# Two float32 transformer blocks on one core: where the projection steps and the reciprocal turns stand inside the attention loops

## The chip, the cores and the metric

The kernel runs on one core of a Trainium2 chip. It is one launch that computes four layers. The metric is the device time of that launch in microseconds (us). The core's engines work side by side and meet only at semaphores: TensorE (PE in the rows, its weight loads PEld), VectorE (DVE), ScalarE (ACT), GpSimd (POOL), and SyncE (SP), which only issues DMAs here.

## The reference

One sequence of 512 tokens of width 1024 passes two blocks of two layers each. Only the attention with 64-wide heads matters here:

```python
# even layer of block 1                      odd layer of block 1: dilated windows, then MLA
qa, ka, va, qd, kd, vd = split_cols(h @ w_in, EVEN_IN_SPLIT)
o_a = moba_attention(heads(qa, 8, 64), heads(ka, 8, 64), heads(va, 8, 64), rel_table[:, :8])
o_b = diff_attention(qd, kd, vd, lam, subln_g, lam_init, ...)   # p[0] - lam * p[1], then rmsnorm of the heads' output
# both layers of block 2
yc = neighbourhood_attention(qc, kc, vc, rpb[l])
gates = jax.nn.sigmoid(gl + b_gate[l]); merged = sum(gates * (ys @ w_branch))
```

In each of them 512 queries meet up to 512 keys, a bias is added, a softmax is taken, and its output is divided by the row sums (`den`). All is float32. A product with a weight is made of three matmuls, of high and low parts: `hh·wh + hl·wh + hh·wl`.

## The kernel before

Every engine's program is written out by hand, and each engine runs its own in the order written. A wait stops everything that stands behind it on that engine.

There are five passes through the function `attention`: moba, diff, dil, and na once in each of two rounds of a loop. A pass has four groups (g = 0 to 3) of two heads and four query tiles, so 32 units. PE, ACT and DVE each count slots t = 0, 1, 2, ... One unit goes through the slots like this:

- PE, even t: `score(t)` and `score(t+1)`, rows `S<-k_sb,q_sb` or `S<-kr_sb,qr_sb`. DVE: bias and row minimum (`biased<-S,...`, L1375). ACT: `soften`, the exponential (`probs<-biased,stats`, L1074), which also waits for PE's transpose of unit t-2.
- PE: transpose of unit t-2 (`T<-ident,probs`, L598). ACT: `copy_turned` of the same unit (`probsT<-T`, L1080), after its `soften(t)`.
- PE, odd units together: the product with V (`O<-probsT,V`, L699; in diff `O<-V,probsT`, L604, each unit for itself).

Between these PE makes the projections for the next group. A **part** is one k step of three matmuls with 512 columns (L470 to L472); eight parts make the queries of the next group in the PSUM bank `PA`, eight more its keys in the bank `PB`. `FILL` says how many parts go into each slot of a group, `last_plan` how many parts of the phase behind (the diff queries and keys, the out projection, the merge gates and the first branch product) go into the slots from 24 on. DVE takes the queries out of PA in the third slot (`take_q`, L1472) and the keys out of PB in the sixth slot (`take_k`, L1477) of the group; `score` of the next group waits for both. When the last part of queries or keys is done, POOL splits the next weights into the free buffer (L450, then L452).

The row sums are inverted token by token, but are wanted along the columns. So at slot `Y_TURN[g]` PE runs `den_turn`: eight pairs of small matmuls (L714) put the reciprocals of group g into a bank, ACT copies the bank one slot later (L1125, "the copy of the reciprocals", `den_copied`), behind its `soften` and `copy_turned` of that slot, DVE multiplies (L1425), ACT and DVE split the result (L1129, L1429). In diff, `y_turn` at the same place transposes the normed output (L724) after DVE's `y_norm` (L1456) in slot 8g + 13.

```python
                for t in range(end + 1):
                    if t < 32 and t % 2 == 0:
                        score(t); score(t + 1)
                    if t in turns:
                        (y_turn if kind == "diff" else den_turn)(b, turns.index(t))
                    for part in parts[sum(slots[:t]):sum(slots[:t + 1])]:
                        part()
```

Of the kernel before, what the change touches and what calls it, by code (L numbers as in the profile page):

```python
# [9 lines left out]
ACT = mybir.ActivationFunctionType  # L10

S = 512
P = 128
DT = 8
# [99 lines left out]

FILL = [3, 3, 2, 2, 3, 3, 0, 0]
Q_AT, K_AT = 3, 6
Y_TURN = {"moba": (15, 23, 27, 35), "diff": (15, 23, 30, 38)}
Y_TURN["dil"] = Y_TURN["na"] = Y_TURN["moba"]

# [70 lines left out]
def build(nc, x_in, weights, consts, cols_in, lam_in, rel_in, rpb_in, strips_rel, strips_na, out):  # L190
    with ExitStack() as ctx:
# [130 lines left out]

        NTABLE, NFIRST = 8, 5

        def flat_y(g):
# [137 lines left out]
        def _(pe):  # L463
# [157 lines left out]

            def qk_parts(b, *bank_free):

                def part(j):
                    if j == DT:
                        pe.wait_ge(*bank_free)
                    qk_part(b, j, j + 1)

                return [lambda j=j: part(j) for j in range(2 * DT)]

            def attention(b, b0, kind, last_parts=(), last_plan=()):
# [5 lines left out]
                parts = sum((qk_parts({**b, **{n: b[n] + m * g for n, m in (("e", 2), ("a", 1), ("b", 1))}},  # L637
                                      *((y_split, 2 * (b["g"] + max(g - 1, 0)) + 1) if kind == "diff" else
                                        (den_copied, b["dc"] + max(g - 1, 0))))
                             for g in range(3)), []) + list(last_parts)  # L640
                slots = FILL * 3 + list(last_plan)
                slots += [0] * (end + 1 - len(slots))
# [61 lines left out]
            def den_turn(b, g):  # L704

                pe.wait_ge(den_ready, b["dr"] + 4 * g + 4)
                if g < 3:
                    pe.wait_ge(pb_taken, b["b"] + min(g + 2, 3) + 1)
                else:
                    pe.wait_ge(o_taken, b["u"] + 24 + 2)  # L710
                for qt in range(QT):
                    for head in range(2):
                        r = rden_of[g % 2][:, 2 * qt + head:2 * qt + head + 1].to_broadcast([P, 64])
                        last = mm((PB if g < 3 else O0)[64 * head:64 * head + 64, qt * P:qt * P + P], r, ident[:, :],  # L714
                                  start=True, stop=True)
                last.then_inc(yt_ready, 2)
# [150 lines left out]
            def gate_part(b, k):  # L867

                if k == 0:
                    pe.wait_ge(pa_taken, b["a"] + 1)  # L870
                    pe.wait_ge(w_split, b["e"] + 3)
                last = three(PA[:, :], wsl(0, k), hs(k), k == 0, k == DT - 1)
                if k == DT - 1:
                    last.then_inc(gate_ready, 1)
# [96 lines left out]
            def moba_stat():  # L971
                pe.wait_ge(table_in, 16 * NTABLE)
                stat(H("moba_v"), False)

            v_projection(H("moba_v"), between=(None, moba_stat, lambda: spread(H("moba_v"))))
            attention(H("moba"), H("moba_q0"), "moba", qk_parts(H("diff_q0"), den_copied, 3),
                      [2, 2, 2, 1, 1, 0, 0, 2, 2, 2, 2])
            v_projection(H("diff_v"))
            o = H("out0")
            first_out = [lambda s=s, k=k: out_part(o, s, k) for s in range(2) for k in range(6)]  # L980
            first_out += [lambda s=s: out_part(o, s, 6) for s in range(2)]
            attention(H("diff"), H("diff_q0"), "diff", first_out, [1, 1, 1, 1, 1, 1, 0, 0, 0, 2, 2, 1, 1, 1, 1])
            out_part(o, 0, 7); out_part(o, 1, 7)
# [10 lines left out]
            qk_part(H("dil_q0"), DT, 2 * DT)  # L994
            attention(H("dil"), H("dil_q0"), "dil")
            pe.wait_ge(kr_done, 1)
# [5 lines left out]
            with pe.Fori(0, LAYERS2) as l:  # L1002
                axial_kv(H("axial_kv", l)); pool_tiles(H("pool", l), H("axial_kv", l), H("axial", l)); axial(H("axial", l))
                qk_part(H("na_q0", l), 0, 2 * DT)
                v_projection(H("na_v", l), True)
                m = H("merge", l)
                first_gate = [lambda k=k: gate_part(m, k) for k in range(DT)] + [lambda k=k: branch_part(m, k) for k in range(4)]
                attention(H("na", l), H("na_q0", l), "na", first_gate, [1] * 12)
                merge(m)
                out_tiles(H("out2", l), lambda k: (mh[:, k, :], ml[:, k, :]), m_split, H("out2", l)["m"], 1)  # L1010
                stat(H("norm_mp", l))
                up(H("up2", l), True); down(H("down2", l))
                stat(H("norm_fp", l))
# [3 lines left out]
        def _(act):  # L1017
# [84 lines left out]
            def attention(b, kind, ytile, early=None):  # L1102
# [3 lines left out]
                for t in range(turns[3] + (2 if kind == "diff" else 4)):  # L1106
# [11 lines left out]
                    if t - 1 in turns:  # L1118
                        g = turns.index(t - 1)
                        act.wait_ge(yt_ready, 2 * (b["g"] + g) + 3)  # L1120
                        if kind == "diff":
                            A(tile(yh, ytile + g), (PB if g < 3 else O0)[:, :], ACT.Copy, scale=scale).then_inc(y_hi, 2)
                        else:
                            act.wait_ge(y_split, 2 * (b["g"] + max(g - 1, 0)) + 1)
                            A(flat_y(g), (PB if g < 3 else O0)[:, :], ACT.Copy).then_inc(den_copied, 1)  # L1125
                    if kind != "diff" and t - 3 in turns:
# [132 lines left out]
        def _(dve):  # L1259
# [219 lines left out]
            def attention(b, kind, ytile, after=None):  # L1479
# [10 lines left out]
                for t in range(turns[3] + (3 if kind == "diff" else 5)):  # L1490
# [20 lines left out]
                    if after is not None and t == 29:  # L1511
                        take_q(after, 0)
                    if after is not None and t == 36:
                        take_k(after, 0)
# [479 lines left out]
```

## Time and profile before

| | |
|---|---|
| median of 3 runs | 3264.05 us (3263.01 to 3266.23) |
| profiled execution: its time | 3260.93 us |
| its span, first to last instruction | 3259.1 us |
| PE busy | 3105.8 us, 95% |
| DVE / ACT / POOL busy | 1481.7 / 788.6 / 1660.0 us |
| mean granted TensorE clock | 0.969 of full speed |
| moba, diff, dil, na, na in the span | from 52, 162, 731, 1547 and 2512 us, 83 to 108 us each |

Times of rows are us from the span's start. An idle time in brackets at a row's end, with a releaser, is how long the engine stood still ahead of it, and what ended that. PE's spans overlap its next instruction's, so a distance is best read from start to start.

### The profile page before, as it was taken

The numbers are of one execution on the slowest core, as the hardware profiler recorded it, in microseconds if no ns is written. First come the engines' busy times: TensorE is split into PE (matmuls) and PEld (weight loads), VectorE is DVE, ScalarE is ACT, GpSimd is POOL, SyncE is SP. The second block draws the span as 40 slices with busy tenths as digits, with TensorE's granted clock in tenths as the row PEclk, the third lists the DMA queues.
The fourth block names the chain that finished last, engine by engine and source line by source line (L and its number), as shares of the span: only waits on it lengthen the run. The fifth ranks groups of instructions, "written<-read, shape, count | busy, mean of one in ns | idle before, by whom it ended". The sixth has DMA issues, their size and how long they took to land.

```text
span 3259.1 us, 44842 instructions
## 1 busy us (share of the span) xinstructions
PE 3105.8 (95%) x14594; PEld 2441.7 (75%) x14594; DVE 1481.7 (45%) x2555; ACT 788.6 (24%) x1425; POOL 1660.0 (51%) x1254
## 2 busy tenths in 40 slices
PE   8998999999899999899999989998899999989997
PEld 6776888876678887667678868887667678868885
DVE  3246444332454433633533476631633433576622
ACT  2343221014322211243421122210142511122201
POOL 4324666662166666312346646665313256646674
PEclk9999999999999999889999989999889999999998
DMA  6251223321022233102312222232102322212232
GB/s 159 78 161 65 94 95 105 105 91 59 26 90 97 97 109 104 36 23 57 93 68 97 87 66 97 96 114 85 40 33 62 75 78 97 90 65 97 97 113 74
DMA packets 99595, 274.79 MB, mean 84 GB/s; under 512 B 38126, under 2 KB 38894, under 8 KB 99490
## 3 DMA queue, kind: packets, MB, share of 16 engines
q1 hardware_dynamic: 97328, 269.07, 25.8%
q10 hardware_dynamic: 2162, 4.36, 0.7%
q8 instruction: 61, 1.00, 0.1%
q14 instruction: 44, 0.36, 0.0%
HBM read 269.66 MB, written 11.54 MB: 86 GB/s over the span
## 4 chain that ended last, share of the span: by engine, by line
PE 71%; DVE 4%; issue 2%; ACT 1%; DVEq 0%; ACTq 0%
PE PA L470 11%; PE PA L471 10%; PE PA L472 10%; PE PB L470 8%; PE PB L472 8%; PE PB L471 8%; PE T L598 2%; PE O L604 2%; PE S L567 2%; PE O L699 1%; PE S L660 1%; PE O L502 1%; DVE hl L1298 1%; DVE tmps L1336 0%; PE PB L759 0%
## 5 line engine op out<-in xcount | busy, mean ns | idle before, releaser
L452 POOL TENSOR_TENSOR wl<-raw,wh 128x1024 fp32r<-128x1024 f32 (+2 forms) x416 | 1126.6, 2708 | 33.4
L449 POOL TENSOR_TENSOR zero<-zero 128x1 f32<-128x1 f32 x416 | 82.7, 199 | 1530.7 <-PE PA L472 799.0
L470 PE MATMUL PA<-hh,wh 128*128 128x512 f32 x1392 | 566.2, 407 | 30.4 <-DVE hl L1298 11.4
L471 PE MATMUL PA<-hl,wh 128*128 128x512 f32 x1392 | 550.1, 395 | 0.0
L472 PE MATMUL PA<-hh,wl 128*128 128x512 f32 x1392 | 549.6, 395 | 0.0
L450 POOL CAST wh<-raw 128x1024 fp32r<-128x1024 f32 (+2 forms) x416 | 476.8, 1146 | 0.0
L470 PEld LDWEIGHTS PA<-hh,wh 128*128 128x128 f32 x1392 | 265.7, 191 | 139.8 <-issue 65.8
L470 PE MATMUL PB<-hh,wh 128*128 128x512 f32 x896 | 358.5, 400 | 0.0
L472 PE MATMUL PB<-hh,wl 128*128 128x512 f32 x896 | 350.4, 391 | 0.0
L471 PE MATMUL PB<-hl,wh 128*128 128x512 f32 x896 | 350.2, 391 | 0.0
L472 PEld LDWEIGHTS PA<-hh,wl 128*128 128x128 f32 x1392 | 266.3, 191 | 57.6
L471 PEld LDWEIGHTS PA<-hl,wh 128*128 128x128 f32 x1392 | 266.4, 191 | 54.0 <-issue 2.2
L1074 ACT ACTIVATE probs<-biased,stats 128x512 f32<-128x512 f32 (+2 forms) x240 | 155.2, 647 | 408.6 <-PE T L598 226.3
L1631 DVE SCALAR_TENSOR_TENSOR tmps<-S,cols,tmps 128x511 f32<-128x511 f32 (+1 forms) x264 | 197.9, 750 | 39.6 <-DVE tmps L1631 19.8
L470 PEld LDWEIGHTS PB<-hh,wh 128*128 128x128 f32 x896 | 169.1, 189 | 47.5 <-issue 14.4
L472 PEld LDWEIGHTS PB<-hh,wl 128*128 128x128 f32 x896 | 168.7, 188 | 36.0
L471 PEld LDWEIGHTS PB<-hl,wh 128*128 128x128 f32 x896 | 169.1, 189 | 33.7 <-issue 1.2
L598 PEld LDWEIGHTS T<-ident,probs 128*128 128x128 f32 x792 | 98.8, 148 | 72.5 <-issue 37.3
L1170 ACT ACTIVATE T<-tmps 128x512 f32<-128x512 f32 x88 | 53.0, 602 | 391.7 <-DVE tmps L1631 391.7
L1298 DVE SCALAR_TENSOR_TENSOR hl<-x,cols,hh 128x512 fp32r<-128x512 f32 (+1 forms) x80 | 129.3, 1622 | 39.0 <-ACT hh L1040 38.8
L470 PE MATMUL PA<-acth,wh 128*128 128x512 f32 x352 | 137.4, 390 | 0.0
L598 PE MATMUL T<-ident,probs 128*128 128x128 f32 x792 | 136.3, 288 | 0.8 <-ACT probsT L1080 0.8
(285 smaller groups left out, 4928.0 us busy)
## 6 DMA issues: line engine op xcount, KB each, us to landing
raw<-in_w_up SPq DMA_DIRECT2D x176, 512.0 KB, 3.4
raw<-in_w_down SPq DMA_DIRECT2D x64, 768.0 KB, 4.2
raw<-in_w_merge SPq DMA_DIRECT2D x48, 768.0 KB, 4.2
raw<-in_w_out SPq DMA_DIRECT2D x32, 512.0 KB, 3.4
strips_na<-in_rpb SPq DMA_DIRECT2D x1, 7620.0 KB, 32.0
raw<-in_w_pool SPq DMA_DIRECT2D x12, 512.0 KB, 3.4
raw<-in_w_na_qk SPq DMA_DIRECT2D x12, 512.0 KB, 3.5
raw<-in_w_na_v SPq DMA_DIRECT2D x8, 512.0 KB, 3.5
```

Of the source, the lines that this page charges most:

```text
L449: nc.gpsimd.tensor_tensor(zero[:, :], zero[:, :], zero[:, :], ALU.add)
L450: nc.gpsimd.tensor_copy(wh[s][:, 0:width], raw[s][:, 0:width]).then_inc(w_head, 1)
L452: nc.gpsimd.tensor_tensor(wl[s][:, 0:width], raw[s][:, 0:width], wh[s][:, 0:width].bitcast(F), ALU.subtract).then_inc(w_split, 1)
L470: mm(dst, h_, rh, start=first, stop=False)
L471: mm(dst, h_, rl, start=False, stop=False)
L472: return mm(dst, l_, rh, start=False, stop=last)
L567: mm(SB[t % 2][:, 0:L], q_sb[r, qt * P:qt * P + P], k_sb[r, 0:L], start=True, stop=True).then_inc(s_ready, 1)
L598: last = nc.tensor.transpose(TB[t % 2][:, k * P:k * P + P], probs[t % 2][:, k * P:k * P + P], ident[:, :])
L604: last = mm(OB[t % 2][:, 0:dv], probsT[t % 2][:, k * P:k * P + P], values(k), start=(k == 0), stop=(k == L // P - 1))
L1074: A(probs[t % 2][:, 0:L], biased[t % 2][:, 0:L], ACT.Exp, scale=-1.0, bias=mn[:, t % 8:t % 8 + 1], accum_out=den[:, t % 8:t % 8 + 1]).then ...
L1298: STT(out=tile(hl, j), in0=tile(x, j), scalar=cols[:, bass.ds(gain_at + j, 1)], in1=tile(hh, j).bitcast(F), op0=ALU.mult, op1=ALU.subtract ...
L1631: ins = STT(out=dst[:, lo:hi], in0=src[:, lo - d:hi - d], scalar=w(k), in1=dst[:, lo:hi], op0=ALU.mult, op1=ALU.add)
```

## The change

Three tables of numbers and the semaphores that go with them. In groups 1 and 2 the parts stand two to a slot and begin in slots 6 and 7 of the group before, which had none (diff keeps one empty slot); `last_plan` begins at slot 22 instead of 24. The reciprocals of groups 0 and 1 are turned in slots 12 and 20 instead of 15 and 23, through PA (the queries' bank) instead of PB, and so the parts that write PA next (queries of group 3 in slot 14, the first part of the phase behind in slot 22) wait for ACT's copy of them. In diff `y_turn` moves from slots 15 and 23 to 16 and 24. DVE's take of the next phase's keys in moba moves from slot 36 to 34.

```diff
-FILL = [3, 3, 2, 2, 3, 3, 0, 0]
+FILL = {"moba": ([3, 3, 3, 3, 2, 2], [2, 2, 2, 2, 2, 2, 2, 2]), "diff": ([3, 3, 3, 3, 2, 2], [2, 2, 2, 2, 0, 3, 3, 2])}
+FILL["dil"] = FILL["na"] = FILL["moba"]
-Y_TURN = {"moba": (15, 23, 27, 35), "diff": (15, 23, 30, 38)}
+Y_TURN = {"moba": (12, 20, 27, 35), "diff": (16, 24, 30, 38)}
...
+        def den_bank(g):
+            return (PA, PA, PB, O0)[g]
...
-            def qk_parts(b, *bank_free):
+            def qk_parts(b, q_free=None, k_free=None):
                 def part(j):
-                    if j == DT:
-                        pe.wait_ge(*bank_free)
+                    if j == 0 and q_free is not None:
+                        pe.wait_ge(*q_free)
+                    if j == DT and k_free is not None:
+                        pe.wait_ge(*k_free)
...
-                                      *((y_split, 2 * (b["g"] + max(g - 1, 0)) + 1) if kind == "diff" else
-                                        (den_copied, b["dc"] + max(g - 1, 0))))
+                                      None if kind == "diff" or g < 2 else (den_copied, b["dc"] + g - 1),
+                                      (y_split, 2 * (b["g"] + g - 1) + 1) if kind == "diff" and g else None)
                              for g in range(3)), []) + list(last_parts)
-                slots = FILL * 3 + list(last_plan)
+                slots = FILL[kind][0] + FILL[kind][1] * 2 + list(last_plan)
...
-                if g < 3:
-                    pe.wait_ge(pb_taken, b["b"] + min(g + 2, 3) + 1)
+                if g < 2:
+                    pe.wait_ge(pa_taken, b["a"] + g + 2 + 1)
+                elif g == 2:
+                    pe.wait_ge(pb_taken, b["b"] + 3 + 1)
...
@@ gate_part (first part of the merge)
                     pe.wait_ge(w_split, b["e"] + 3)
+                    pe.wait_ge(den_copied, b["dc"] - 2)
...
-            attention(H("moba"), H("moba_q0"), "moba", qk_parts(H("diff_q0"), den_copied, 3),
-                      [2, 2, 2, 1, 1, 0, 0, 2, 2, 2, 2])
+            attention(H("moba"), H("moba_q0"), "moba", qk_parts(H("diff_q0"), (den_copied, 2), (den_copied, 3)),
+                      [2, 2, 1, 1, 1, 1, 0, 2, 2, 2, 2])
...
-            attention(H("diff"), H("diff_q0"), "diff", first_out, [1, 1, 1, 1, 1, 1, 0, 0, 0, 2, 2, 1, 1, 1, 1])
+            attention(H("diff"), H("diff_q0"), "diff", first_out, [1, 1, 1, 1, 0, 1, 0, 1, 0, 0, 0, 2, 2, 1, 1, 1, 1])
...
-            attention(H("dil"), H("dil_q0"), "dil")
+            attention(H("dil"), H("dil_q0"), "dil", (), [0, 0])
...
-                attention(H("na", l), H("na_q0", l), "na", first_gate, [1] * 12)
+                attention(H("na", l), H("na_q0", l), "na", first_gate, [2, 2, 1, 1, 1, 1, 0, 1, 1, 1, 1])
...
-                    if after is not None and t == 36:
+                    if after is not None and t == 34:
                         take_k(after, 0)
```

How PE's order changes at three places, row by row of the program (in brackets the semaphores that a row waits for; `S` are the scores, `T` the transposes of the exponentials, `O` the products with V). First, in moba, PE before, from the scores of slot 14 to the first part of slot 16:

```order
L660 MATMUL S<-kr_sb,qr_sb 128x512 [waits s_taken] x2
L598 MATMUL T<-ident,probs 128x128 [waits pt_copied,p_ready]
L598 MATMUL T<-ident,probs 128x128 x2
L699 MATMUL O<-probsT,V 64x128 [waits pt_copied]
L699 MATMUL O<-probsT,V 64x128 x3
L714 MATMUL PB<-ident,stats 64x128 [waits pb_taken,den_ready]
L714 MATMUL PB<-ident,stats 64x128 x7
L598 MATMUL T<-ident,probs 128x128 [waits pt_copied,p_ready]
L598 MATMUL T<-ident,probs 128x128 x2
L660 MATMUL S<-k_sb,q_sb 128x128 [waits s_taken,pb_taken,pa_taken]
L660 MATMUL S<-k_sb,q_sb 128x128 [waits s_taken]
L470 MATMUL PA<-hh,wh 128x512 [waits w_split,pa_taken]
```

and PE of the change in moba, from the last part of slot 13 to the two parts of slot 14:

```order
L474 MATMUL PB<-hh,wh 128x512
L475 MATMUL PB<-hl,wh 128x512
L476 MATMUL PB<-hh,wl 128x512
L602 MATMUL T<-ident,probs 128x128 [waits pt_copied,p_ready]
L602 MATMUL T<-ident,probs 128x128
L666 MATMUL S<-kr_sb,qr_sb 128x512 [waits s_taken] x2
L474 MATMUL PA<-hh,wh 128x512 [waits w_split,pa_taken,den_copied]
L475 MATMUL PA<-hl,wh 128x512
L476 MATMUL PA<-hh,wl 128x512
L474 MATMUL PA<-hh,wh 128x512
L475 MATMUL PA<-hl,wh 128x512
L476 MATMUL PA<-hh,wl 128x512
```

The turn of the reciprocals is gone from slot 15 (it stands in slot 12 now), and slot 14, which had no part, has two, the first of which waits for `den_copied`.

Second, in diff, PE before, slots 14 and 15 up to the first score of slot 16:

```order
L660 MATMUL S<-kr_sb,qr_sb 128x512 [waits s_taken] x2
L598 MATMUL T<-ident,probs 128x128 [waits pt_copied,p_ready]
L598 MATMUL T<-ident,probs 128x128 x2
L604 MATMUL O<-V,probsT 128x128 [waits o_taken,pt_copied]
L604 MATMUL O<-V,probsT 128x128
L724 MATMUL PB<-ident,y_tok 128x128 [waits pb_taken,y_normed]
L724 MATMUL PB<-ident,y_tok 128x128 x3
L598 MATMUL T<-ident,probs 128x128 [waits pt_copied,p_ready]
L598 MATMUL T<-ident,probs 128x128 x2
L604 MATMUL O<-V,probsT 128x128 [waits o_taken,pt_copied]
L604 MATMUL O<-V,probsT 128x128 x2
L660 MATMUL S<-k_sb,q_sb 128x128 [waits s_taken,pb_taken,pa_taken]
```

and of the change, slot 14 and the first rows of slot 15:

```order
L666 MATMUL S<-kr_sb,qr_sb 128x512 [waits s_taken] x2
L474 MATMUL PA<-hh,wh 128x512 [waits w_split,pa_taken]
L475 MATMUL PA<-hl,wh 128x512
L476 MATMUL PA<-hh,wl 128x512
L474 MATMUL PA<-hh,wh 128x512
L475 MATMUL PA<-hl,wh 128x512
L476 MATMUL PA<-hh,wl 128x512
L602 MATMUL T<-ident,probs 128x128 [waits pt_copied,p_ready]
L602 MATMUL T<-ident,probs 128x128 x2
L608 MATMUL O<-V,probsT 128x128 [waits o_taken,pt_copied]
L608 MATMUL O<-V,probsT 128x128
L474 MATMUL PA<-hh,wh 128x512
```

Behind the scores of slot 14 now come two parts of the queries, in slot 15 two more, and they wait for nothing that DVE does in slots 13 to 15; the turn (`PB<-ident,y_tok`) stands behind the scores of slot 16.

Third, in na, PE before at the end of the pass: the transpose of unit 31 (slot 33), a part and the products of units 30 and 31 (slot 34), the last turn and the last part (slot 35):

```order
L598 MATMUL T<-ident,probs 128x128 [waits pt_copied,p_ready]
L598 MATMUL T<-ident,probs 128x128 x3
L470 MATMUL PB<-yh,wh 128x512
L471 MATMUL PB<-yl,wh 128x512
L472 MATMUL PB<-yh,wl 128x512
L699 MATMUL O<-probsT,V 64x128 [waits pt_copied]
L699 MATMUL O<-probsT,V 64x128 x7
L714 MATMUL O<-ident,stats 64x128 [waits o_taken,den_ready]
L714 MATMUL O<-ident,stats 64x128 x7
L470 MATMUL PB<-yh,wh 128x512
L471 MATMUL PB<-yl,wh 128x512
L472 MATMUL PB<-yh,wl 128x512
```

and of the change, from the transpose of unit 30 (slot 32) on:

```order
L602 MATMUL T<-ident,probs 128x128 [waits pt_copied,p_ready]
L602 MATMUL T<-ident,probs 128x128 x3
L705 MATMUL O<-probsT,V 64x128 [waits pt_copied]
L705 MATMUL O<-probsT,V 64x128 x7
L680 REGISTER_ALU
L602 MATMUL T<-ident,probs 128x128 [waits pt_copied,p_ready]
L602 MATMUL T<-ident,probs 128x128 x3
L705 MATMUL O<-probsT,V 64x128 [waits pt_copied]
L705 MATMUL O<-probsT,V 64x128 x7
L723 MATMUL O<-ident,stats 64x128 [waits o_taken,den_ready]
L723 MATMUL O<-ident,stats 64x128 x7
L899 REGISTER_ALU
```

No part is left between the products of units 28 and 29 and the end; the part that stood behind the last turn stands ahead of it now.

## Rows read from the trace of the kernel before

**Rows 1.** The page's head: each engine's busy time, share of the span and instructions.

```profile
PE 3105.8 (95%) x14594; PEld 2441.7 (75%) x14594; DVE 1481.7 (45%) x2555; ACT 788.6 (24%) x1425; POOL 1660.0 (51%) x1254
```

**Rows 2.** Timeline of moba, slots 13 to 15: start, us, engine, line, operation [idle before].

```profile
88.92 0.36 ACT L1080 ACTIVATE probsT<-T 128x256 f32<-128x256 f32 x1
...
89.20 0.55 PE L598 MATMUL T<-ident,probs 128*128 128x128 f32 x3
...
90.75 1.09 PE L714 MATMUL PB<-ident,stats 128*64 128x128 f32 x16 [0.42 <-DVE k_sb L1477]
```

**Rows 3.** Timeline of diff, slots 13 to 16, the turn of slot 23, and slot 29.

```profile
199.33 1.13 PE L660 MATMUL S<-kr_sb,qr_sb 64*128 64x512 f32 x4
...
199.35 3.78 DVE L1456 TENSOR_SCALAR y_tok<-y_tok,stats 128x128 f32<-128x128 f32 x4
...
200.06 2.35 POOL L452 TENSOR_TENSOR wl<-raw,wh 128x1024 fp32r<-128x1024 f32 x1
...
204.51 0.47 ACT L1080 ACTIVATE probsT<-T 128x384 f32<-128x384 f32 x1
...
204.96 1.05 PE L724 MATMUL PB<-ident,y_tok 128*128 128x128 f32 x4 [2.80 <-DVE k_sb L1477]
...
208.54 0.50 PE L470 MATMUL PA<-hh,wh 128*128 128x512 f32 x1
...
232.19 0.97 PE L724 MATMUL PB<-ident,y_tok 128*128 128x128 f32 x4 [2.78 <-DVE kr_sb L1477]
...
248.27 1.25 DVE L1456 TENSOR_SCALAR y_tok<-y_tok,stats 128x128 f32<-128x128 f32 x4
```

**Rows 4.** Stretches behind diff's first turn and na's gap: busy us by engine, PE's granted clock, DMA.

```profile
205.00:208.40 3.40, 3.40 (x17) 3.14 (x17) 1.02 (x5) 1.19 (x3) 0.00 (x0) 0.50 0.39 99
...
2614.80:2621.70 6.90, 6.14 (x15) 4.81 (x16) 1.32 (x3) 2.00 (x2) 3.34 (x1) 0.51 0.33 103
```

**Rows 5.** Timeline of the second na, slots 28 to 35 and the merge's first matmul.

```profile
2599.01 0.50 PE L470 MATMUL PA<-hh,wh 128*128 128x512 f32 x1
...
2599.67 0.59 ACT L1125 ACTIVATE y_tok<-PB 128x512 f32<-128x512 f32 x1
...
2599.81 0.60 PE L598 MATMUL T<-ident,probs 128*128 128x128 f32 x4
...
2606.61 1.09 PE L699 MATMUL O<-probsT,V 128*64 128x128 f32 x16 [0.32 <-ACT probsT L1080]
...
2607.79 0.60 ACT L1080 ACTIVATE probsT<-T 128x512 f32<-128x512 f32 x1 [1.24 <-PE O L699]
...
2609.73 1.09 PE L699 MATMUL O<-probsT,V 128*64 128x128 f32 x16
...
2610.66 1.04 PE L714 MATMUL O<-ident,stats 128*64 128x128 f32 x16
...
2615.56 0.79 PE L470 MATMUL PA<-hh,wh 128*128 128x512 f32 x1 [2.95 <-DVE tmps L1670]
```

**Rows 6.** Timeline of moba, slots 28 and 29, and the two parts of slot 33.

```profile
127.14 0.44 PE L598 MATMUL T<-ident,probs 128*128 128x128 f32 x2
...
127.82 0.59 ACT L1125 ACTIVATE y_tok<-PB 128x512 f32<-128x512 f32 x1
...
134.46 0.50 PE L470 MATMUL PB<-hh,wh 128*128 128x512 f32 x1
...
135.96 0.60 PE L598 MATMUL T<-ident,probs 128*128 128x128 f32 x4
```

**Rows 7.** Timeline of the second na, slots 13 and 14.

```profile
2555.97 0.72 ACT L1074 ACTIVATE probs<-biased,stats 128x512 f32<-128x512 f32 x1 [2.12 <-PE T L598]
...
2556.69 0.57 ACT L1080 ACTIVATE probsT<-T 128x512 f32<-128x512 f32 x1
...
2556.86 0.66 PE L598 MATMUL T<-ident,probs 128*128 128x128 f32 x4
```

**Rows 8.** Timeline of dil, slot 24.

```profile
800.57 1.09 PE L699 MATMUL O<-probsT,V 128*64 128x128 f32 x16 [0.61 <-ACT probsT L1080]
```

More of the change, by code:

```diff
@@ L706, in den_turn @@
                 pe.wait_ge(den_ready, b["dr"] + 4 * g + 4)
-                if g < 3:
-                    pe.wait_ge(pb_taken, b["b"] + min(g + 2, 3) + 1)
+                if g < 2:
+                    pe.wait_ge(pa_taken, b["a"] + g + 2 + 1)
+                elif g == 2:
+                    pe.wait_ge(pb_taken, b["b"] + 3 + 1)
                 else:
                     pe.wait_ge(o_taken, b["u"] + 24 + 2)
+                bank = den_bank(g)
                 for qt in range(QT):
@@ L713, in den_turn @@
                         r = rden_of[g % 2][:, 2 * qt + head:2 * qt + head + 1].to_broadcast([P, 64])
-                        last = mm((PB if g < 3 else O0)[64 * head:64 * head + 64, qt * P:qt * P + P], r, ident[:, :],
-                                  start=True, stop=True)
+                        last = mm(bank[64 * head:64 * head + 64, qt * P:qt * P + P], r, ident[:, :], start=True, stop=True)
                 last.then_inc(yt_ready, 2)
@@ L1124, in attention @@
                             act.wait_ge(y_split, 2 * (b["g"] + max(g - 1, 0)) + 1)
-                            A(flat_y(g), (PB if g < 3 else O0)[:, :], ACT.Copy).then_inc(den_copied, 1)
+                            A(flat_y(g), den_bank(g)[:, :], ACT.Copy).then_inc(den_copied, 1)
                     if kind != "diff" and t - 3 in turns:
```

## Prediction

> **What bounds the kernel now.** I read the page's head first: PE is busy 95% of the span, DVE 45%, ACT 24%, POOL 51% [rows 1]. So only PE's idle time can be won, and every new wait of PE is lost. The timelines of the passes say where the idle time stands and what ends it.
>
> In moba PE stops 0.42 us ahead of the turn in slot 15, for DVE's take of the keys out of PB [rows 2], and as long ahead of slot 23's; dil has the same two. Na has none. In diff the stop in the same places is 2.80 and 2.78 us. The reason stands in two rows there: DVE's `y_norm`, four instructions that take 1.25 us in slot 29, takes 3.78 us in slot 13, while POOL's split of weights (released by the last key part of slot 13) runs from 200.06 to 202.41 [rows 3]. From 205.0 to 208.4 PE is then granted 0.50 of its clock, the 1.2 GHz level [rows 4], and for as long behind the second stop.
>
> The end of na is bound otherwise. PE's last turn starts at 2610.66, ACT and DVE then finish the output, and the merge's second gate projection waits 2.95 us for DVE and starts at 2615.56 [rows 5]. What counts there is when the last turn starts: 4.90 us later the merge goes on. The part behind the turn is free.
>
> **The change part by part**, as the difference of PE's time. A part alone in its slot costs 0.80 us (2599.01 to 2599.81) [rows 5], two cost 1.50 us (134.46 to 135.96) [rows 6]. So a further part costs 0.70 us, and a block of parts has 0.10 us of its own; since PE changes from scores or products to transposes without a block too, I take 0.06 us for a block more. For the waits ACT's order decides: in the slot behind a turn it does `soften`, which waits for PE's transpose in that slot, then `copy_turned`, then the copy of the reciprocals.
>
> *Slot 14 (turn in 12), a new wait for that copy.* In na `copy_turned` of slot 13 ends at 2556.69 + 0.57 = 2557.26 [rows 7]; the copy of a bank takes 0.59 us [rows 5] and ends at 2557.85. PE comes to the place of the part at 2556.86 [rows 7]. Wait: 1.0 us. In moba, with shorter rows: 88.92 + 0.36 + 0.59 = 89.87 against 89.20 [rows 2], 0.67 us; dil the same.
>
> *Slot 22 (turn in 20)*: the same pattern, 1.0 us in na, 0.67 us in moba, nothing in dil, which has no part there.
>
> *Slot 29 (turn in 27, as before)*: PB is written here now instead of in slots 31 (moba) and 32 (na). Moba: the copy ends at 127.82 + 0.59 = 128.41, some 0.1 us on PE sees it, and PE was there at 127.14 [rows 6]: 1.37 us. Na: 2599.67 + 0.59 + 0.1 = 2600.36 against 2599.01 [rows 5]: 1.35 us.
>
> *The end of moba and na, without parts behind slot 32.* The products of units 28 and 29 end at 2606.61 + 1.09 = 2607.70; two copies of 0.60 us must follow before those of 30 and 31 can start, near 2609.0, and PE has one transpose of 0.60 us to do. Idle: 0.7 to 0.9 us, 0.8 taken. Two parts cover it now, and the products start at 2609.73 [rows 5].
>
> *The part behind na's last turn* goes ahead of it: 0.68 us on the path, where it was free.
>
> *Removed*: 0.84 us of stops ahead of the turns in moba and in dil [rows 2], 0.32 us in na (at 2606.61) [rows 5].
>
> *Dil's end* has no parts, and PE waits there for ACT. With the turn of slot 23 gone ahead, the copy of the reciprocals (0.59 us) leaves ACT's slot 24, where PE stood 0.61 us [rows 8]. I take 0.5 us of gain, with bounds of 0 and 1.2 us (both of that copy's and its split's ACT time).
>
> *Diff.* The parts of slots 14 and 15 have another bank and other weights than the stopped turn, so they run while DVE stands. `y_norm` will still meet POOL, since the last key part stays in slot 13; it begins later than now (its ACT work follows a transpose with one part more ahead of it), so it ends some 0.5 us later. From 199.33 [rows 3] I count: scores 1.06, two parts 1.50, transpose and product 1.1, two parts 1.50, transpose 0.5; then the product of unit 12 needs ACT's copy, now done at 204.51 + 0.47 = 204.98, then at 205.5; product, scores and turn bring PE to 207.6. Now the same, without the four parts, is done at 208.54 [rows 3]. Gain: 0.9 + 3.0 = 3.9 us, the slow clock's 1.7 us among it. In slots 22 and 23 only two parts stand in the way, PE waits about 1.9 us for the product of unit 20, and the same count gives 2.4 us. Against that, the key parts of slot 19 wait for DVE's read of the turned output, which is one slot nearer (0.5 us, an estimate by the lengths above; bounds 0 and 1), and 0.1 us of blocks. Diff: 5.7 us won.
>
> Here a rule of the Trainium skill bears. The trace shows `y_norm` stretched to 1 us behind the end of POOL's L452 at 202.41 [rows 3]. "SBUF — State Buffer", section "Who interferes with whom", says that a `tensor_scalar` in a two-port mode and a GpSimd instruction take a shared port pair as an exclusive lock, and the later one blocks for the whole of the other. By that rule the stall stays, and only its cover changes; the trace agrees.
>
> **The sum.** Blocks of parts: moba 27 to 32, dil 18 to 22, na 29 to 32 ahead of the last turn.
> Moba: 2 × 0.67 + 1.37 + 0.8 + 0.3 − 0.84 = +3.0 us.
> Dil: 0.67 + 0.24 − 0.84 − 0.5 = −0.4 us.
> Na: 1.0 + 1.0 + 1.35 + 0.8 + 0.68 + 0.18 − 0.32 = +4.7 us, twice +9.4 us.
> Diff: −5.7 us.
> Together +6.3 us. The profiled execution took 3260.93 us, 1.8 us more than its span, and would take 3267. The median of before is 3264.05, 3.1 us above it; added to that, the sum gives 3270. I say 3269.5, since each wait was counted in full.
>
> All else keeps its cover: the splits of weights that the parts of slots 6 and 14 need are released in slots 2 and 9, and a split takes under 4 us of POOL where four slots take ten; DMAs move with them; DVE and ACT are less than half busy, and while PE waits they catch up.
>
> **Rivals.**
> *The new waits are hidden* (not slower). If ACT were ahead of PE in slots 13, 21 and 28, the waits for `den_copied` would fall out: 3 × 0.67 + 1.37 + 2 × (2.0 + 1.35) = 10.1 us less, so 3264 − 4 = 3260. For it: ACT stands idle 2.12 us ahead of `soften` [rows 7]. Against it: that idle time is a wait for PE's own transpose, and the copy stands behind it in order. It decides from the point where PE has 2 us of work between that transpose and the part; it has the scores, 1.06 us.
> *The clock falls behind the new gaps* (slower still). In diff it fell during gaps of 2.8 us, and once in the 2.95 us gap ahead of the merge, for 6.9 us [rows 4, 5]; the first na kept it. Without the part behind the last turn both gaps are 3.9 us. A fall costs half its time: 1.7 us in diff, 3.4 us in na; one more in na and one in diff that stays make 3270 + 5 = 3275. The Trainium skill, "TensorE: Matmul & The Clock Gate", section "HAM oscillation", says likewise that idle gaps bring the lower level and half the time spent in it is lost; by its rule the first na too would lose its 3.4 us. The trace agrees in three gaps, not in the fourth.
> *Diff gains nothing*: if the parts of slots 14 and 15 waited for weights, or the later turn held DVE back as much as it is relieved, −5.7 becomes 0 and the time 3275. Against it: the weights' split has five slots.
>
> **How the numbers follow.** My forecast (waits as counted, diff covered) 0.5, between 3265 and 3273 by the bounds of dil's end, of slot 19 and of the passes' ends. Waits hidden, wholly or in good part: 0.25, 3257 to 3264. Clock falls: 0.15. Diff gains nothing: 0.1. The range that leaves out 2 in 10 is 3259 to 3276. A measurement of this kernel tells 0.2% (6.5 us) from no change. Slower by more is nearly half of the forecast's share and most of the two slower rivals': 0.42. Faster by more needs the hidden waits and more from diff: 0.15. Within: 0.43.
>
> **What would show it.** Right: rows of PE that write PA in slots 14 and 22 and PB in slot 29 with idle time ahead, ended by ACT's copy, 0.7 to 1.4 us each; no 2.8 us stop in diff and full clock at its first turn; na's last turn some 4.7 us later after the pass's first score; a gap near 3.9 us ahead of the merge. Wrong: those rows without idle time; a turn in slot 12 that waits for the take of the queries; passes of moba and na that end sooner than before.

## The result, and the profile after

The changed kernel takes 3269.86 us (median of 22 runs, 3264.14 to 3274.83); the kernel before took 3265.10 us beside it (22 runs, 3263.01 to 3269.27). The ratio is 1.0014, with a 95% interval of 1.0008 to 1.0021: 4.8 us slower, inside the 0.2% that I called no change. Forecast were 3269.5 us, in a range of 3259 to 3276.

The page's head, as in [rows 1]. PE's busy share has not moved:

```profile
span 3268.5 us, 44834 instructions
PE 3109.4 (95%) x14594; PEld 2443.0 (75%) x14594; DVE 1474.3 (45%) x2555; ACT 788.9 (24%) x1425; POOL 1658.0 (51%) x1254
```

The lines behind the diff stand 4 to 9 numbers further down now: L470 is L474, L699 L705, L714 L723, L724 L732, L1125 L1134, L1375 L1384, L1456 L1465, L1670 L1679.

*Moba.* Timeline, slots 14, 29 and the last products (start, us, engine, line, operation, [idle before and what ended it]). The places are those of [rows 2] and [rows 6]:

```profile
89.63 0.59 ACT L1134 ACTIVATE y_tok<-PA 128x512 f32<-128x512 f32 x1
90.27 0.50 PE L474 MATMUL PA<-hh,wh 128*128 128x512 f32 x1 [0.56 <-ACT y_tok L1134]
...
127.89 0.59 ACT L1134 ACTIVATE y_tok<-PB 128x512 f32<-128x512 f32 x1
128.52 0.50 PE L474 MATMUL PB<-hh,wh 128*128 128x512 f32 x1 [1.41 <-ACT y_tok L1134]
...
139.78 1.09 PE L705 MATMUL O<-probsT,V 128*64 128x128 f32 x16 [0.69 <-ACT probsT L1089]
```

The 0.42 us stop ahead of the turn is gone. In its place the first part behind the turn waits until ACT has copied the reciprocals out of the same bank, in slots 14 and 22 (0.56 us each) and 29. Slot 29 is the dearest, since the copy starts only at 127.89 and PE has stood there since 127.11.

*Second na.* Timeline of the same places, as in [rows 7] and [rows 5]; the last row is the merge's second gate projection:

```profile
2565.89 0.49 PE L474 MATMUL PA<-hh,wh 128*128 128x512 f32 x1 [0.95 <-ACT y_tok L1134]
...
2611.77 0.50 PE L474 MATMUL PB<-yh,wh 128*128 128x512 f32 x1 [1.23 <-ACT y_tok L1134]
...
2619.37 1.09 PE L705 MATMUL O<-probsT,V 128*64 128x128 f32 x16 [0.32 <-ACT probsT L1089]
...
2621.74 1.09 PE L705 MATMUL O<-probsT,V 128*64 128x128 f32 x16 [0.69 <-ACT probsT L1089]
...
2622.66 1.04 PE L723 MATMUL O<-ident,stats 128*64 128x128 f32 x16
...
2627.47 0.49 PE L474 MATMUL PA<-hh,wh 128*128 128x512 f32 x1 [3.76 <-DVE tmps L1679]
```

The merge still follows 4.81 us behind the last turn (4.90 before, from 2610.66 to 2615.56 [rows 5]), and the part that stood in between now stands ahead of the turn: the gap grew from 2.95 to 3.76 us and gained nothing.

*Diff.* Timeline, slots 13 to 15, and the turn for slot 23's old place, against [rows 3]:

```profile
200.90 3.43 DVE L1465 TENSOR_SCALAR y_tok<-y_tok,stats 128x128 f32<-128x128 f32 x4
200.91 2.38 POOL L456 TENSOR_TENSOR wl<-raw,wh 128x1024 fp32r<-128x1024 f32 x1
...
206.23 0.94 PE L608 MATMUL O<-V,probsT 128*128 128x128 f32 x6 [0.81 <-ACT probsT L1089]
...
229.93 0.94 PE L608 MATMUL O<-V,probsT 128*128 128x128 f32 x6 [1.49 <-ACT probsT L1089]
...
231.21 0.66 PE L732 MATMUL PB<-ident,y_tok 128*128 128x128 f32 x4
```

DVE's `y_norm` is still stretched (3.43 us against 3.78), but PE has four parts to do meanwhile, and its stop of 2.80 us is one of 0.81. In the second place two parts cover less, and 1.49 us stay (beside 0.48 us at 226.70).

*The clock.* Windows (from:to, length, busy us of each engine with its instructions, granted clock, DMA share, GB/s):

```profile
205.00:208.40 3.40, 2.59 (x20) 2.07 (x19) 2.84 (x14) 2.37 (x6) 0.00 (x0) 1.00 0.39 131
...
259.60:263.00 3.40, 2.93 (x6) 1.83 (x6) 1.48 (x3) 0.20 (x1) 1.23 (x3) 0.50 0.00 0
809.20:812.60 3.40, 3.40 (x31) 3.07 (x28) 0.00 (x0) 0.26 (x1) 0.00 (x0) 0.50 0.00 0
1655.70:1659.10 3.40, 3.40 (x10) 2.64 (x9) 0.69 (x1) 1.79 (x2) 0.00 (x0) 0.50 0.00 0
```

205.0 to 208.4 was at half clock before [rows 4] and is at full clock now, and so is the stretch behind diff's second stop. But new falls (stretches in which the granted clock is at the lower level) came behind diff's last turn, at the end of dil, and behind the gap ahead of the first na's merge. All stretches at half clock add up to 202.6 us before and 205.5 us now. Their places are not fixed: in a second profile of the same changed kernel ("after, again" below) the windows at 259.6 and 809.2 us are at full clock, behind diff's last turn stands one such stretch instead of two, and the sum is 201.8 us.

Three times are useful below for each kernel: the time; the *full-clock time*, span times mean granted clock, as a mean over its runs; and the rest of the span, *lost to the clock* (an upper bound, since a low clock costs nothing where PE stands still anyway). For the same reason the split is not clean: the last run below has 3.4 us more full-clock time than its work explains, while less is lost to the clock. Differences under some 3 us are not to be read from it. Before: 3156.8 + 106.3 us. After: 3165.6 + 102.4 us. So by this split the change costs 8.8 us of work and waits, and 4 us came back from the clock.

### The profile page after: what moved, and what is told of

It reads as the page before. It is cut to its first block, busy times and chain, and to the rows that moved or that the text cites. A ratio compares the mean times of both kernels' runs of the same rounds, so it can differ in the third digit from the quotient of the medians.

```text
span 3268.5 us, 44834 instructions
## 1 busy us (share of the span) xinstructions
PE 3109.4 (95%) x14594; PEld 2443.0 (75%) x14594; DVE 1474.3 (45%) x2555; ACT 788.9 (24%) x1425; POOL 1658.0 (51%) x1254
## 4 chain that ended last, share of the span: by engine, by line
PE 71%; DVE 4%; issue 2%; ACT 2%; DVEq 0%; ACTq 0%
PE PA L474 11%; PE PA L475 10%; PE PA L476 10%; PE PB L474 8%; PE PB L475 8%; PE PB L476 8%; PE T L602 2%; PE O L608 2%; PE S L571 2%; PE O L705 1%; PE S L666 1%; PE O L506 1%; DVE hl L1307 0%; DVE tmps L1345 0%; ACT probsT L1089 0%
## 5 line engine op out<-in xcount | busy, mean ns | idle before, releaser
L474 PE MATMUL PA<-hh,wh 128*128 128x512 f32 x1392 | 568.1, 408 | 37.3 <-DVE hl L1307 11.2
L474 PEld LDWEIGHTS PA<-hh,wh 128*128 128x128 f32 x1392 | 266.9, 192 | 149.3 <-issue 69.0
L474 PE MATMUL PB<-hh,wh 128*128 128x512 f32 x896 | 359.4, 401 | 1.9 <-ACT y_tok L1134 1.4
L474 PEld LDWEIGHTS PB<-hh,wh 128*128 128x128 f32 x896 | 168.9, 189 | 50.6 <-issue 15.5
L474 PE MATMUL PA<-acth,wh 128*128 128x512 f32 x352 | 137.4, 390 | 0.0
L476 PE MATMUL PA<-acth,wl 128*128 128x512 f32 x352 | 137.0, 389 | 0.0
```

Of the source, the lines that this page charges most:

```text
L474: mm(dst, h_, rh, start=first, stop=False)
L476: return mm(dst, l_, rh, start=False, stop=last)
```

## Experiments

All start from the changed kernel. Ratios are to the kernel before, run on the same chip beside it (3265.1 to 3265.3 us in the first eight runs, 3263.1 in the last two, where 103.7 us of it were lost to the clock).

| run | time, us | ratio (95%) | full-clock time | lost to the clock |
|---|---|---|---|---|
| before | 3265.1 | 1 | 3156.8 | 106.3 |
| after | 3269.9 | 1.0014 (1.0008 to 1.0021) | 3165.6 | 102.4 |
| diff's tables alone | 3258.1 | 0.9979 (0.9970 to 0.9987) | 3153.1 | 103.0 |
| all but diff's | 3280.8 | 1.0040 (1.0027 to 1.0053) | 3168.1 | 109.5 |
| late turn | 3270.7 | 1.0009 (1.0000 to 1.0018) | 3157.1 | 109.6 |
| tail back | 3267.6 | 1.0003 (0.9995 to 1.0012) | 3158.6 | 106.1 |
| late turn, tail back | 3258.0 | 0.9980 (0.9971 to 0.9989) | 3154.4 | 102.1 |
| early turn | 3257.8 | 0.9975 (0.9966 to 0.9984) | 3155.1 | 101.6 |
| diff's keys sooner | 3261.5 | 0.9987 (0.9978 to 0.9996) | 3155.4 | 104.0 |
| after, again | 3268.8 | 1.0013 (1.0004 to 1.0022) | 3165.5 | 101.6 |
| early turn, tail back | 3256.4 | 0.9978 (0.9969 to 0.9987) | 3151.8 | 102.1 |
| four matmuls more | 3265.7 | 1.0008 (0.9999 to 1.0017) | 3169.9 | 93.1 |

**Diff alone, and all but diff.** First only diff's tables are the new ones (the diff below; turns in `PB` and last plans of the others as before), then only the others':

```diff
-FILL = {"moba": ([3, 3, 3, 3, 2, 2], [2, 2, 2, 2, 2, 2, 2, 2]), "diff": ([3, 3, 3, 3, 2, 2], [2, 2, 2, 2, 0, 3, 3, 2])}
+FILL = {"moba": ([3, 3, 2, 2, 3, 3, 0, 0], [3, 3, 2, 2, 3, 3, 0, 0]), "diff": ([3, 3, 3, 3, 2, 2], [2, 2, 2, 2, 0, 3, 3, 2])}
...
-Y_TURN = {"moba": (12, 20, 27, 35), "diff": (16, 24, 30, 38)}
+Y_TURN = {"moba": (15, 23, 27, 35), "diff": (16, 24, 30, 38)}
```

> Diff alone has the new tables; moba, dil and na stand as before. Waits theory: diff's pass from its first score to its last turn is 94 us long instead of 101, nothing else changes, so the time is 7 us under before, 3258. Clock theory (the gain of diff is only the two falls of the clock, which come back elsewhere): half of that or less, 3261 to 3264.

> The change without its diff part. Waits theory: the 2.80 us stops of diff are back, everything else as in the changed kernel: 7 us over the changed kernel, 3277, 12 over before. Clock theory: 3271 to 3274.

3258.1 us, as the waits theory had it, and 3280.8 us (five executions only), which is above both expectations. Beside the kernel before (3265.3 us) diff's part gains 7 us and the rest costs 15.5 us. About half of diff's gain is the clock's: −3.7 us of full-clock time and −3.3 us lost to the clock. Of the rest's cost 3.2 us are the clock's (109.5 against 106.3 us). In full-clock time the two parts, −3.7 and +11.3 us, come to +7.6 us where the whole has +8.8, which is as near as the split allows.

**Late turn.** The even parts stay, but the reciprocals of groups 0 and 1 are turned in `PB` at 15 and 23 again. No part waits for the copy in slots 14 and 22.

```diff
-Y_TURN = {"moba": (12, 20, 27, 35), "diff": (16, 24, 30, 38)}
+Y_TURN = {"moba": (15, 23, 27, 35), "diff": (16, 24, 30, 38)}
-            return (PA, PA, PB, O0)[g]
+            return (PB, PB, PB, O0)[g]
```

> The changed kernel with even parts, but with the reciprocals of moba, dil and na turned in slots 15 and 23 through the keys' bank as before. Waits theory: the waits ahead of the first part of slots 14 and 22 are gone (0.62 us twice in moba, once in dil, 1.0 and 0.95 us in each na: 5.8 us), and no 0.42 us stop comes back at the turn, since two parts stand ahead of it in slot 14: 3264. Spread theory (the even spread itself costs, by its blocks): no change against the changed kernel, 3270.

**Tail back.** The last parts of moba and na stand in slots 31 to 35 again:

```diff
-                      [2, 2, 1, 1, 1, 1, 0, 2, 2, 2, 2])
+                      [2, 2, 1, 1, 1, 1, 0, 0, 0, 2, 2, 2, 2])
-                attention(..., "na", first_gate, [2, 2, 1, 1, 1, 1, 0, 1, 1, 1, 1])
+                attention(..., "na", first_gate, [2, 2, 1, 1, 1, 1, 0, 0, 0, 0, 1, 1, 1, 1])
```

> The changed kernel with the same parts in slots 22 to 27, but the last ones moved from slots 29 to 32 back to slots 31 to 34 in moba and 32 to 35 in na. Waits theory: the wait of slot 29 (1.4 us in moba, 1.3 in na) and the idle time at the end (0.7 us in each) go, and one part lies behind na's last turn again: 2.1 us in moba, 2.7 us in each na, together 7.6 us less than the changed kernel, 3262. The gap ahead of the merge is 3 us again instead of 3.76. Spread theory: no change, 3270. Clock theory: less only as far as the clock falls less often.

**Both.**

> The new tables for diff, the even parts, but the turns of moba, dil and na in slots 15 and 23 through the keys' bank and the last parts in slots 31 to 35. Waits theory: all new waits are gone (5.8 + 7.6 us under the changed kernel), and the 0.42 us stops of before too: 3256 to 3257, under diff alone by 1 to 2 us. Spread theory: the blocks cost 3 to 4 us, so 3261 or more.

Each remedy alone missed: 3270.7 and 3267.6 us where 3264 and 3262 were expected; by its time the late turn looks as if the spread theory were right. Together they gave 3258.0 us. The traces tell a part of the reason. With the late turn the waits of slots 14 and 22 are gone and of ACT's copy only slot 29's is left, here moba's (one stop of 0.42 us for DVE came back, at dil's second turn). This kernel's lines stand 2 lower:

```profile
125.66 0.50 PE L474 MATMUL PB<-hh,wh 128*128 128x512 f32 x1 [1.41 <-ACT y_tok L1132]
```

The full-clock times fell by 8.5, 7.0 and 11.2 us, where 5.8, 7.6 and 13.4 us of waits were counted: the right size, but not additive to better than 4 us. What grew is the time lost to the clock: 109.6 us with the late turn and 106.1 with the tail back, against 102.4. Some of the stretches at half clock lie far from any edit. Two windows between the two na passes, in code that is the same in both kernels; first the changed kernel, then the late turn:

```profile
2451.60:2461.80 10.20, 9.52 (x63) 7.11 (x63) 3.80 (x17) 7.25 (x14) 0.00 (x0) 1.00 0.00 0
```

```profile
2451.60:2461.80 10.20, 10.20 (x34) 7.06 (x33) 3.26 (x12) 5.24 (x9) 0.00 (x0) 0.50 0.00 0
```

At full clock PE does 63 matmuls there, at half clock 34. This stretch alone does not set the late turn apart, though: with the tail back too the same code is at half clock again (2442.0 to 2452.2 us there), and yet only 102.1 us are lost. Why one remedy alone loses more than both together stays open. That the clock makes the difference, the eleven runs of the late turn do say: four at a mean clock of 0.968 to 0.969 took 3261 to 3265 us, seven at 0.964 to 0.966 took 3270 to 3275 us.

One more thing stands in these numbers. With both remedies the kernel has diff's new tables and the even parts everywhere, and takes 3258.0 us; diff's tables alone took 3258.1. I had expected 1 to 2 us less. From first score to last turn moba is 1.4 us shorter than with diff alone (85.1 against 86.5 us), each na 0.9 us longer (99.4 against 98.5). So the even spread outside diff gained nothing in the time, even without its waits.

**Early turn.** Instead of later, the turns come one slot sooner, with a take of the queries that is one slot sooner too; all else as changed.

```diff
-Y_TURN = {"moba": (12, 20, 27, 35), ...
+Y_TURN = {"moba": (11, 19, 26, 35), ...
-                    if t < 24 and t % 8 == Q_AT:
+                    if t < 24 and t % 8 == (Q_AT if kind == "diff" else 2):
```

> The changed kernel with the turns of moba, dil and na one slot earlier still, 11, 19 and 26, with the queries taken one slot earlier to free the bank. One slot lies between ACT's copy and the next part in that bank, so by the waits theory all waits for the copy go (0.62 x 3 + 1.5 + 2 x 3.3 = 10 us): 3260. The idle time at the passes' ends stays. If the wait does not come from the distance between copy and part, nothing changes: 3270.

3257.8 us: 12 less than the changed kernel, and 11 less than its repeat (3268.8 us below), which ran beside it on the same chip. The copy is now two slots ahead of the part. Timeline of the second na, where the part behind the copy no longer waits:

```profile
2562.61 0.59 ACT L1134 ACTIVATE y_tok<-PA 128x512 f32<-128x512 f32 x1
...
2565.06 0.50 PE L474 MATMUL PA<-hh,wh 128*128 128x512 f32 x1
```

From its first to its last score this na takes 91.4 us, the changed one 94.7. Of the waits on ACT's copy none is left in the list of PE's waits. From first score to last turn moba takes 86.5 us before, 88.6 in the changed kernel and 85.6 here; the second na takes 98.6, 103.7 and 100.4 us. So the waits were all that made moba slower, and most of what made na so; na's last 1.8 us are those of its end, which this edit leaves. (The profiled execution was the slowest of the eleven, 3267.9 us with 226.8 us at half clock. The passes compared here hold no half-clock stretch.)

**Diff's keys sooner.** On top of late turn and tail back, diff's key parts end a slot sooner, so that POOL's split starts ahead of `y_norm`; diff's turns are back at 15 and 23.

```diff
-... "diff": ([3, 3, 3, 3, 2, 2], [2, 2, 2, 2, 0, 3, 3, 2])}
+... "diff": ([3, 3, 3, 3, 2, 2], [2, 2, 2, 2, 3, 3, 2, 0])}
```

> As the kernel with late turns and moved ends, but in diff the keys' parts of groups 1 and 2 end one slot sooner (slots 10 to 12 and 18 to 20) and diff's turns stand in slots 15 and 23 again. Port theory (y_norm is stretched by the split of weights that the last key part releases): the split ends some 1.4 us sooner against y_norm, whose four instructions take 2 us or less together instead of 3.4, and the remaining waits of 0.8 and 1.5 us in diff shrink by over 1 us: 1 to 2 us less than without it. Else y_norm stays at 3.4 us.

3261.5 us, 3.5 more where I had expected 1 to 2 less. `y_norm` did become shorter (1.68 us against 3.44), but the turn waits for DVE's take of the keys again. Timeline of DVE, POOL and PE in diff; first late turn and tail back, then with the keys sooner:

```profile
196.47 3.44 DVE L1463 TENSOR_SCALAR y_tok<-y_tok,stats 128x128 f32<-128x128 f32 x4
196.48 2.38 POOL L456 TENSOR_TENSOR wl<-raw,wh 128x1024 fp32r<-128x1024 f32 x1
```

```profile
196.40 2.36 POOL L456 TENSOR_TENSOR wl<-raw,wh 128x1024 fp32r<-128x1024 f32 x1
198.12 1.68 DVE L1463 TENSOR_SCALAR y_tok<-y_tok,stats 128x128 f32<-128x128 f32 x4
200.80 0.68 DVE L1484 TENSOR_TENSOR k_sb<-PB,rs 128x512 f32<-128x512 f32 x1
201.62 0.63 PE L731 MATMUL PB<-ident,y_tok 128*128 128x128 f32 x4 [0.70 <-DVE k_sb L1484]
```

`y_norm` ends 1.0 us behind POOL's split in both (199.91 against 198.86, 199.80 against 198.76), whenever it began. The pass is 1.1 us longer from first score to last turn (95.1 against 94.0 us), by the stop of 0.70 and 0.69 us ahead of its two turns. So where `y_norm` lies matters less than that parts stand behind it and the turn comes late.

**The changed kernel again**, for its own spread:

> The changed kernel once more, beside the others on the same chip: 5 us over before, 3270, for comparison.

3268.8 us, with the ratio, the full-clock time and the time lost within 1 us of the first 22 runs: the difference to the kernel before repeats.

**Early turn and tail back.**

> The changed kernel with both remedies that cost least: the turns of moba, dil and na in slots 11, 19 and 26 (as in the run with the early turn), and the last parts of moba and na back in slots 31 to 35. If the waits for ACT's copy and the idle ends are all there is, the early turn leaves three idle ends of 0.7 us and two parts of 0.68 us ahead of na's last turn, which go here: 3.4 us less work than in the run with the early turn (3257.8 us), so 3254 us, and na from its first to its last score about 2 us shorter than the 91.4 us there. If clock falls undo it, as they did in the runs with one remedy alone, the pass lengths still shrink so, and the time stays at 3256 to 3262.

The waits fell as counted: 3.3 us less full-clock time than with the early turn alone, the lowest of all. The time is 3256.4 us, or 0.9978 against 0.9975 by the ratios: no gain that a measurement shows. The first to the last score of na came down by 0.6 us only, not the 2 us that I wrote; the rest of the saving stands behind the last score, where the gap ahead of the merge is 2.95 us again.

**Four matmuls more.** A small push in time: the first matmul of diff's V projection is issued five times over.

```diff
-            v_projection(H("diff_v"))
+            v_projection(H("diff_v"), again=4)
+                            for _ in range(again if k == 0 and t == 0 else 0):
+                                mm(banks[t][:, :], hh[:, k, c], W[0], start=True, stop=True)
```

> The changed kernel with four matmuls more (the first of diff's V projection issued five times over, 0.23 us each, 0.9 us in all), whose results are overwritten: everything behind them starts 0.9 us later and nothing else differs. If the time at the slow clock depends only on what work there is, the half-clock time in the profile stays at 202 to 206 us and the time is 3270 to 3271. If it depends on where in time the gaps of PE lie as well, the half-clock time between the two na passes (71.7 us in the changed kernel, 81.9 us in the run with the late turn, the same code in both) can go up by 10 us for a shift this small, and the time is off by several us from the 0.9 us that the added work takes: 3273 to 3278, with all pass lengths at full clock unchanged.

Its passes are as long as the changed kernel's at full clock, from first to last score (diff 78.7 us, na 94.8 and 94.7; moba takes 80.2 us with 3.4 us of them at half clock, so 78.5 at full clock), but the kernel became no slower: 3265.7 us, a ratio of 1.0008 (0.9999 to 1.0017), which by its interval can't be told from the changed kernel's 1.0014. What did move is the clock. The stretches at half clock add up to 187.8 us instead of 205.5, and over all runs 93.1 us are lost to the clock instead of 102.4 (103.7 instead of 106.3 for the kernel before beside it, so some 7 of the 9 us are this kernel's own). Both of my numbers were wrong: the half-clock time moved by far more than 3 us, and it moved down. Full-clock time rose by 4.3 us for 0.9 us of work.

Between the na passes the half-clock time stayed at 71.7 us. Stretches went missing at 259, 809, 945 and 1478 us; the first two are missing from the changed kernel's second profile as well, so the added matmuls need not be their cause. And one came in moba, behind slot 29's wait of 1.41 us. It ends 11 us ahead of the added matmuls (142.2 us), which therefore can't have made it. The changed kernel is at full clock there; the profile of all but diff's tables has the same stretch:

```profile
127.60:131.00 3.40, 3.40 (x10) 2.38 (x12) 0.67 (x1) 0.12 (x1) 0.48 (x1) 0.50 0.47 147
```

The stretch at 1478 us lies in a window that the four matmuls don't touch; first the changed kernel, then with four matmuls more:

```profile
1478.20:1488.40 10.20, 10.20 (x34) 7.11 (x34) 3.26 (x12) 5.20 (x9) 0.00 (x0) 0.50 0.00 0
```

```profile
1478.20:1488.40 10.20, 9.04 (x56) 6.66 (x56) 5.64 (x18) 4.55 (x11) 0.00 (x0) 1.00 0.00 0
```

## Why the prediction was right, and where its terms were not

The direction and the time came out, and those of moba, diff and na by the mechanisms named. The terms one by one; a stage is measured from the first score of a pass to the first score of the next.

*The waits for the copy (slots 14, 22 and 29).* Right. Moba 0.56, 0.56 and 1.41 us against 0.67, 0.67 and 1.37; na 0.95, 0.88 and 1.23 us against 1.0, 1.0 and 1.35. The early turn, which takes only these away, is 11 to 12 us faster than the changed kernel, where they add up to 9.2 us: the rival that they are hidden has fallen. That diff gains nothing fell with diff's tables alone.

*The ends of moba and na.* Right. 0.69 us against 0.8. But na's stop of 0.32 us, which I had removed, is still there at 2619.37, since na's parts there are single ones as before.

*The spread itself in moba.* Too dear. Moba's stage grew by 2.1 us and not by 3.0. I had charged each block of parts 0.06 us and seen no gain. Rows of before and after at the first scores of group 1 (slot 8):

```profile
69.70 1.02 PE L660 MATMUL S<-kr_sb,qr_sb 64*128 64x128 f32 x4
...
70.23 0.29 PEld L660 LDWEIGHTS S<-kr_sb,qr_sb 64*128 64x128 f32 x2 [0.24 <-DVE stats L1375]
```

```profile
72.38 0.49 PE L666 MATMUL S<-kr_sb,qr_sb 64*128 64x128 f32 x4
```

Before, slots 6 and 7 held no part, PE reached these scores ahead of DVE, and the second pair, those of the second head, had to wait until DVE had read the scores in that head's bank (1.02 us in all). With parts ahead of them all four start within 0.22 us and take 0.49. That is 0.5 of the missing 0.9 us. Another 0.3 us are the waits and the end, which came out shorter than counted; 0.1 us is left.

*Na.* 4.7 us predicted each; 5.2 us from first score to last turn (98.6 to 103.7 us), and 6.7 us to the next pass's first score in the first round, 1.7 of it the fall behind the merge's gap. The terms that failed are the stop of 0.32 us above and 0.6 us that no term names: with the measured waits in their places and the stop kept, the sum is 4.6 us.

*Dil.* −0.4 us predicted, no change found at full clock. The copy's wait came in slot 14 (0.56 us at 769.05). The gain in the place of [rows 8] did come, 0.61 us of idle time are gone there. But with the turn out of slot 23, PE is at the scores of slot 24 before DVE is:

```profile
793.42 0.48 PE L666 MATMUL S<-kr_sb,qr_sb 64*128 64x128 f32 x2 [0.64 <-DVE stats L1384]
```

*Diff.* −5.7 us predicted, −7.4 from first score to last turn (101.3 to 93.9 us). 3.4 of them are the two falls, as I had them; the rest is 4.0 us where I had 2.3. ACT's copy that the product of unit 12 waits for ends at 206.18, or 204.3 on the scale of before (this pass starts 1.9 us later), where I had counted 205.5: I let `y_norm` begin 0.5 us later, and it began 0.35 us sooner and took 3.43 us, not 3.78. But two falls came back behind the last turn, at 259.6 and 266.4, and diff's whole stage, up to dil's first score, gained 5.2 us. The Trainium skill, "SBUF — State Buffer", section "Who interferes with whom", agrees in the main: of `y_norm`'s four instructions the one that meets the split took 2.47 us in the changed kernel and 2.40 in the one before, and one that meets none takes 0.29 us; with the keys sooner DVE went on at POOL's end too, though it had begun later. The section also gives the ports to whoever issues first. The rows don't show that: DVE's starts 0.01 us ahead of POOL's in two of them (200.90 against 200.91, 196.47 against 196.48), and DVE is the one that is held.

*The clock.* The step that came right by luck. I took the two falls in diff off as a gain of 3.4 us and gave new falls a rival of their own. In the profile the gain is nil: falls went in diff and came in diff, dil and the first na's stage, there behind the gap of 3.76 us, as that rival said; the second na's stage has fewer (35.9 us against 43.6). Over all runs, though, the changed kernel loses 4 us less to the clock than the one before, and the variants lie between 93 and 110 us. This term is nearly as large as the whole difference measured, and I had its size right only by luck. I had also given the new waits no clock cost of their own, and the stretch behind slot 29's wait in moba, with four matmuls more, suggests that they can have one. The Trainium skill, "TensorE: Matmul & The Clock Gate", section "HAM oscillation", ties the falls to idle gaps; the changed kernel's first na agrees (a gap of 3.76 us, and half clock from 1655.7), but the windows at 1478 and 2451 us show falls that come and go with no edit near them. Nor does the length of the gap ahead of the merge settle it: with 2.95 us the clock fell behind neither of the two gaps in the profile of diff's tables alone, behind one in that of the kernel before, and behind both in those of the tail back and of both remedies. What decides there stays open.

The sum in other words: +6.3 us forecast, with 3.4 us of clock in it, so +9.7 us of work and waits; measured, by the split of the table, 8.8. The clock gave back 4.0 instead of 3.4 us.

## What to carry to other kernels

When a result is turned through a bank that projections also use, ask first when the copy out of that bank ends against when the next write comes. The same turn was a loss in one slot, hidden one slot sooner, and harmless in the bank that is idle. Parts that cover a stall belong right behind what is late, and parts ahead of the last turn of a pass are paid in full where they were free behind it. With edits worth a few microseconds, split each run into its full-clock time and what the clock took before believing a difference: two remedies looked useless until that was done. The split itself is good to some 3 us, so run the unchanged kernel again and a combination of the remedies as well; here the early turn and the two remedies together showed in the plain time what each alone did not.

## What I had not expected of the hardware

Some stretches of 3.4 to 10.2 us at the 1.2 GHz level appear and vanish in code that no edit touches. The profiles have 202.6 us of them in all before, 230.1 with the late turn, 187.8 with 0.9 us of useless matmuls added, and 205.5 and 201.8 us in two profiles of one and the same kernel, not all in the same places. And two score matmuls on 64 rows each ran side by side: four of them took 0.49 us together when they were issued in one go, and 1.02 us when the second pair came behind a wait.
